# Gate and up products of six of the eight expert quads in one 512-column matmul, with the sigmoid behind both, in an fp32 mixture-of-experts block on one core

## What is computed

```python
def hierarchical_moe(x, w_router_group, w_router_expert, w_gate, w_up, w_down):
    ...
    h = (jax.nn.silu(jnp.einsum('td,edf->tef', xt, w_gate))
         * jnp.einsum('td,edf->tef', xt, w_up)
         * combine[..., None].astype(x.dtype))
    return jnp.einsum('tef,efd->td', h, w_down).reshape(nb_, s_, d_)
```

## Time and profile before

| | us |
|---|---|
| median of three runs | 392.3 |
| the profiled execution, its own time | 392.49 |
| its span in the trace | 390.2 |
| TensorE busy | 358.6 (92%) |
| VectorE busy | 161.3 (41%) |
| ScalarE busy | 138.0 (35%) |
| moved by DMA | 132.79 MB, mean 340 GB/s |

### The profile page before, as it was taken

The page is one execution under the profiler, slowest core; times in us unless marked ns, Lnnn a source line. Parts: engine busy times, 40 slices in busy tenths (PEclk is TensorE's granted clock), DMA queues, the critical chain, the costliest instruction groups (busy, mean ns, idle before and its releaser), DMA issues.

```text
span 390.2 us, 8014 instructions
## 1 busy us (share of the span) xinstructions
PE 358.6 (92%) x3331; PEld 284.4 (73%) x3331; DVE 161.3 (41%) x337; ACT 138.0 (35%) x240; POOL 35.2 (9%) x42
## 2 busy tenths in 40 slices
PE   7999999999999999999899999999599398299995
PEld 7999988999999999998657575656256156157642
DVE  3546579797465656464730303030610111010235
ACT  4643565655535444435723131322112113012012
POOL 3310000000000000001000005207711000000001
PEclk9999999999999999999999999999899699599999
DMA  8699884966759889799899999999999999999962
GB/s 281 204 329 373 302 280 160 349 221 217 269 180 306 279 264 376 228 392 375 306 365 429 425 422 427 425 419 423 426 423 413 427 427 427 427 426 425 412 245 108
DMA packets 52053, 132.79 MB, mean 340 GB/s; under 512 B 2818, under 2 KB 36626, under 8 KB 41012
## 3 DMA queue, kind: packets, MB, share of 16 engines
q1 hardware_dynamic: 51572, 131.88, 87.7%
q0 software_dynamic: 304, 0.17, 0.2%
q10 hardware_dynamic: 144, 0.26, 0.2%
HBM read 131.25 MB, written 1.05 MB: 339 GB/s over the span
## 4 chain that ended last, share of the span: by engine, by line
PE 67%; DMA 16%; SPq 8%; DVE 5%; ACT 2%; issue 1%; DVEq 0%; ACTq 0%
PE bank L1200 15%; DMA gu<-in_w_up 14%; PE bank L1494 10%; PE bank L1229 8%; PE bank L1362 6%; PE bank L1530 6%; PE bank L1232 4%; PE bank L1445 4%; PE bank L1542 4%; SPq L469 4%; SPq L434 3%; PE bank L1344 3%; PE bank L1299 2%; DMA raw<-in_w_in 2%; DVE wl L835 2%
## 5 line engine op out<-in xcount | busy, mean ns | idle before, releaser
L835 DVE TENSOR_TENSOR wl<-raw,wh 128x1024 fp32r<-128x1024 f32 x54 | 65.8, 1223 | 55.0 <-ACT wh L653 54.8
L1494 PE MATMUL bank<-gu,xg 128*32 128x256 f32 x1024 | 61.8, 401 | 20.4 <-DMA gu<-in_w_up 19.8
L653 ACT ACTIVATE wh<-raw 128x1024 fp32r<-128x1024 f32 x54 | 56.5, 1056 | 59.8 <-DMA raw<-in_w_in 20.2
L1494 PEld LDWEIGHTS bank<-gu,xg 128*32 128x32 f32 x1024 | 33.4, 116 | 45.4 <-issue 25.0
L1229 PE MATMUL bank<-xh,wh 128*128 128x256 f32 x176 | 44.1, 288 | 0.5 <-ACT qT L715 0.5
L1229 PE MATMUL bank<-xl,wh 128*128 128x256 f32 x176 | 43.1, 283 | 0.0
L1229 PEld LDWEIGHTS bank<-xh,wh 128*128 128x128 f32 x176 | 33.6, 191 | 2.7 <-issue 2.0
L1097 DVE TENSOR_SCALAR xg<-bank,gcol,bcol 128x128 f32<-128x128 f32 x32 | 10.9, 404 | 59.0 <-PE bank L1445 59.0
L1229 PEld LDWEIGHTS bank<-xl,wh 128*128 128x128 f32 x176 | 33.7, 191 | 0.0
L1445 PEld LDWEIGHTS bank<-pick,x1p 128*128 128x128 f32 x256 | 29.8, 192 | 1.9 <-issue 0.9
L1445 PE MATMUL bank<-pick,x1p 128*128 128x128 f32 x256 | 30.2, 276 | 0.6 <-DVE pick L1068 0.6
(11 more groups left out here) (234 smaller groups left out, 588.7 us busy)
## 6 DMA issues: line engine op xcount, KB each, us to landing
gu<-in_w_up SPq DMA_DIRECT2D x31, 1024.0 KB, 19.6
gu<-in_w_gate SPq DMA_DIRECT2D x30, 1024.0 KB, 15.0
dn<-in_w_down SPq DMA_DIRECT2D x26, 1024.0 KB, 17.6
raw<-in_w_in SPq DMA_DIRECT2D x40, 512.0 KB, 5.6
raw<-in_w_o SPq DMA_DIRECT2D x8, 512.0 KB, 5.0
raw<-in_w_out_conv SPq DMA_DIRECT2D x4, 512.0 KB, 4.0
raw<-in_w_out_attn SPq DMA_DIRECT2D x4, 512.0 KB, 5.0
gu<-in_w_gate SPq DMA_DIRECT2D x1, 2048.0 KB, 10.7
```

Source lines behind the costliest of these rows:

```text
L653: act.activation(wh[:, s, :].rearrange("p (k c) -> p k c", k=KC), raw[pair % NRAW][:, :].rearrange("p (k c) -> p k c", k=KC) [:, :, n % 2 ...
L835: dve.tensor_tensor(wl[:, s, :].rearrange("p (k c) -> p k c", k=KC), raw[pair % NRAW][:, :].rearrange("p (k c) -> p k c", k=KC) [:, :, n % ...
L1494: mm = pe.matmul(bank[6 - part][g, 0:DE], xg[:, k, g], w[:, e, part, k, :], start=(k == 0), stop=(k == KC - 1), skip_group_check=True)
```

## The change

In rounds 1 to 6 each chunk and expert gets one matmul of 512 moving columns, gate and up side by side, where there were two of 256; the result fills all of `bank[6]`, gate in its first half and up in its second. Rounds 0 and 7 keep the separate products, but their up half goes to the second half of `bank[6]` too. `gate_ps` is signalled in round 0 alone (for SyncE's loads of quad 2). The sigmoid waits for `gu_ps`, both products, in every round. VectorE reads the up product from `bank[6]`.

```diff
--- before.py
+++ after.py
@@ -780,7 +780,7 @@
 
             def compute(n):
 
-                act.wait_ge(gate_ps[-1], n)
+                act.wait_ge(gu_ps, n)
                 act.activation(sg[:, :], bank[6][:, 0:DE], ACT.Sigmoid).then_inc(sg_done, 1)
                 act.wait_ge(hT_ps, n)
                 act.activation(hT[:, :, :], bank[4][:, 0:SEQ].rearrange("p (j s) -> p j s", j=FC),
@@ -1124,7 +1124,7 @@
                                   ALU.mult).then_inc(round_link, 1)
                 dve.wait_ge(round_link, 2 * c + 2)
                 dve.wait_ge(gu_ps, c + 1)
-                dve.tensor_tensor(hs[:, :], sg[:, :], bank[5][:, 0:DE],
+                dve.tensor_tensor(hs[:, :], sg[:, :], bank[6][:, DE:2 * DE],
                                   ALU.mult).then_inc(bank_free[6], 1)
                 dve.wait_ge(put_ps, c + 1)
                 pick_slots(coming)
@@ -1473,32 +1473,52 @@
                             pe.wait_ge(gu_in[half], 16 * QE * (2 * loads - (half == 0 and loads > 1)))
                         if q == 2:
                             pe.wait_ge(gate2_in, 16 * len(GATE_PARTS))
-                        for part in range(2):
-                            if last_quad:
+                        def gathered(k):
+
+                            if k < KC // 2:
+                                pe.wait_ge(xg_a, KC // 2 * c + k + 1)
+                            else:
+                                pe.wait_ge(xg_v, KC // 2 * c + k - KC // 2 + 1)
+
+                        def project(k, parts):
+
+                            for e in range(QE):
+                                g = slice(SLOTS * e, SLOTS * (e + 1))
+                                mm = pe.matmul(bank[6][g, parts.start * DE:parts.stop * DE], xg[:, k, g],
+                                               w[:, e, parts, k, :],
+                                               start=(k == 0), stop=(k == KC - 1), skip_group_check=True)
+                            return mm
+
+                        if 0 < q < NQ - 1:
+                            for k in range(KC):
+                                gathered(k)
+                                mm = project(k, slice(0, 2))
+                            mm.then_inc(gu_ps, 1)
+                        elif q == 0:
+                            for i, (lo, hi) in enumerate(GATE_PARTS):
+                                if hi == KC:
+                                    pe.wait_ge(rank_read, 1)
+                                    gather(c, [NK - 1])
+                                for k in range(lo, hi):
+                                    gathered(k)
+                                    mm = project(k, slice(0, 1))
+                                mm.then_inc(gate_ps[i], 1)
+                            for k in range(KC):
+                                mm = project(k, slice(1, 2))
+                            mm.then_inc(gu_ps, 1)
+                        else:
+                            for part in range(2):
                                 for e in range(QE):
                                     pe.wait_ge(last_gu_in[part][e], 16)
                                     if part and e < QE - 1:
                                         stay_warm(WARM_LAST[e])
-                            for k in range(KC):
-                                if last_quad and part == 1 and k == KHALF:
-                                    pe.wait_ge(last_up_end, 16)
-                                if q == 0 and part == 0 and k == KHALF:
-                                    pe.wait_ge(rank_read, 1)
-                                    gather(c, [NK - 1])
-                                if part == 0 and k < KC // 2:
-                                    pe.wait_ge(xg_a, KC // 2 * c + k + 1)
-                                elif part == 0:
-                                    pe.wait_ge(xg_v, KC // 2 * c + k - KC // 2 + 1)
-                                for e in range(QE):
-                                    g = slice(SLOTS * e, SLOTS * (e + 1))
-                                    mm = pe.matmul(bank[6 - part][g, 0:DE], xg[:, k, g],
-                                                   w[:, e, part, k, :],
-                                                   start=(k == 0), stop=(k == KC - 1), skip_group_check=True)
-                                for i, (_, hi) in enumerate(GATE_PARTS):
-                                    if part == 0 and k == hi - 1:
-                                        mm.then_inc(gate_ps[i], 1)
-                            if part == 1:
-                                mm.then_inc(gu_ps, 1)
+                                for k in range(KC):
+                                    if part and k == KHALF:
+                                        pe.wait_ge(last_up_end, 16)
+                                    if not part:
+                                        gathered(k)
+                                    mm = project(k, slice(part, part + 1))
+                            mm.then_inc(gu_ps, 1)
                         pe.wait_ge(pickw_done, 2 * c + 2)
                         for t in range(TT):
                             mm = pe.transpose(bank[7][:, SEQ + t * P:SEQ + (t + 1) * P],
```

## The result

The changed kernel is slower by 0.46% (ratio 1.0046, 95% interval 1.0034 to 1.0058): median 394.16 us of 20 runs against 392.4 us of 20 runs of the kernel before, +1.8 us (+1.3 to +2.3). The forecast was 393.5, +1.24. The profiled execution took 393.78 us, span 391.5.

What follows compares the result with a forecast made beforehand. Expert-weight loads run without a gap to about 378 us; from 365.8 us compute sets the end. Round 6 +0.52, round 7 +0.87, late weights -0.15 make +1.24 us: from 392.3 to 393.5 us, range 392.4 to 394.9.

Steps and rivals of the forecast that it cites:

- The sigmoid behind both products adds 0.87 us a round, and the wide product takes back 0.07: Every round: sigmoid and first multiplication lie between product and `hs`, +0.87 us; 512-column products save 0.07 in rounds 1 to 6.
- The 2.6 us less a round: Wide product: estimate from the Trainium skill's matmul spacing, 4.5 us instead of 7.11; the sum went by the rows instead.
- The table load stays free: ScalarE's table load in the loop (1.28 us) still runs ahead of the sigmoid's wait and adds nothing.
- the rival of the dry queue: SyncE's issue at 247.06: queue empties if rounds 0 to 2 grow over 4.3 us; +4.5 us, 396.8, chance 0.05.
- Round 7, +0.87 less what late weights give back (+0.72): Last round: late sigmoid and multiplication on the path, +0.87 us; less waiting for the last down weights, -0.15.
- Round 6, +0.52: Round 6 lasts 0.80 us longer, TensorE has 0.28 to spare, so the last up product starts 0.52 us later.
- The first rival: Only round 7 counts: TensorE has more to spare at the last up weights, round 6's term vanishes; 393.0 us, chance 0.27.
- Rounds 0 to 5, "Cost 0": Longer rounds are absorbed by idle time before round 4; the later load issue still finds 1.9 us of loads queued; 0 us.
- a digit below 9: Sign against the forecast: DMA's busy digit dropping below 9 in a slice from the 21st to the 38th.

Runs made afterwards that it cites:

- e2: The kernel before with the sigmoid waiting for the end of the up product in rounds 0, 1 and 2 alone: +1.5 us against the kernel before.
- e1: The changed kernel with the 512-column products of rounds 1 to 6 split again into two of 256, sigmoid still behind both: +2.6 us against the kernel before.
- e4: The kernel before with the sigmoid waiting for the end of the up product in round 7 alone: +0.9 us against the kernel before.
- e3: The kernel before with the sigmoid waiting for the end of the up product in rounds 3 to 6 alone: +0.2 us against the kernel before.
- e7: The changed kernel without the six filling matmuls behind the third up load of round 7: +0.8 us against the kernel before.
- e8: The kernel before without the six filling matmuls behind the third up load of round 7: -0.3 us against the kernel before.
- e6: The kernel before with one of quad 4's gate loads (1 MB) issued earlier, ahead of quad 3's down weights: -0.4 us against the kernel before.

## Why the prediction was right and wrong

**Right in the range and the sign** (393.5 forecast, 394.16 measured, in 392.4 to 394.9), and half right in the reason. That the range holds is partly luck. The prediction left out the largest term; had the 1.5 us of e2 come on top of its 1.24 in full, the time would have been 395.0, just outside the range.

- *The sigmoid behind both products adds 0.87 us a round, and the wide product takes back 0.07*: the round's period went from 19.63 us (the sigmoids at 218.62 and 238.25 before) to 20.39, +0.76; expected +0.80. The mechanism is right, and each size is a little off: the late sigmoid adds 0.80 (e1's period of 20.43 against 19.63), because the sigmoid follows the product by 0.03 us and not by the 0.10 that was taken to cancel, and the saving was 0.04. The 2.6 us less a round that the prediction set beside its sum are not in these fp32 rows.
- *The table load stays free*: right, 213.97, ahead of the wait. The drain that the rival of the dry queue mentions does not show: before, the load at 198.45 ends at 199.73, and the sigmoid starts at 199.75.
- *Round 7, +0.87 less what late weights give back (+0.72)*: right for the execution that it was read from, +0.71 there (0.80 less 0.09), and e4 has +0.9. The same term is 0.06 to 0.80 from trace to trace, as the down weights land; the prediction took one value. It also read only the wait at the last down weights (0.40); there is another of 0.54 us at the piece before.
- *Round 6, +0.52*: the mechanism is right, the filling matmuls close up. The up product starts 0.57 us later in the profile, but 0.27 of that is round 6's own later start (339.34 after 339.07), so round 6 gave 0.30, with a product that was 0.16 shorter. Its worth in the timed runs is uncertain, +0.2 in e3 and 0.7 by e7 and e8. The first rival's doubt, that the 0.28 us of slack is one execution's, is borne out by e4 and e6 (none, and 0.64).
- *Rounds 0 to 5, "Cost 0"*: **this is the step that failed.** The working said that the issue at 247.06 had 4.3 us to spare, because `dn_r` landed at 251.4, and that with 2.47 us more "1.9 us of loads" would still be queued. The delay was right: counted from round 0's table load, the issue comes at 50.93 us instead of 48.61, 2.32 us later. The margin was wrong. A landing tells when a load's last part is done, not when the stream of data thins out, and an issue is not yet data: the hole opened over three microseconds before that landing and closed some two microseconds behind the issue. The rival "the load queue runs dry" had the right place and the right mechanism, but the wrong point from which it decides (4.3 us of delay, so only with the table load), and so it got 0.05 and a price of 4.5 us. What it costs at 2.3 us of delay is 1.4 us of loads, and e2 has +1.5. The sign that the prediction had named for this, a digit below 9, did not come, and the mean share from 200 to 360 us stayed at 1.01 (421 GB/s after 424): both were too coarse to see it.

In place of the forecast's sum, the profiled pair has 1.13 (later loads) + 0.30 (round 6) + 0.71 (round 7) = 2.14 us for the experts' part. The timed runs have 1.5 for the hole and 0.2 to 0.7 for round 6; 0.9 for round 7 stands for a kernel without the hole, and behind the hole less of it is left, down to the 0.06 that e2's trace leaves. Added up in full they make 2.6 to 3.1, more than the 1.8 measured; with 0.06 for round 7 they make 1.8 to 2.3. Against that speaks e1, with 2.6 and no wide product. How the rest divides between the overlap, chance and the wide product (0.04 us a round by the rows, 0.6 to 0.8 by the timed runs, whose intervals overlap) stays open. That the profiled executions differ by 1.29, so near to the 1.24 of the forecast, is a coincidence: the changed kernel's started its experts' part 0.86 us early.

## What to carry to other kernels

Read the margin of a load queue from GB/s in windows of a microsecond, not from the last landing, and least of all from a busy digit of a long slice; then keep one more load queued than the landing asks for. Costs measured one by one do not simply add where a late load stands behind them: each hides in the wait that another one causes. A consumer moved behind two producers instead of one costs its own time wherever the chain behind it is waited for, and besides the end of the kernel that includes every place where this chain releases a buffer whose reload is issued just in time. Where matmuls are already spaced by their columns, as here (7.11 and 7.07 us), halving their number gains next to nothing by the rows.

## What the runs showed that was not expected

A load of 1 MB that lands 2.7 us after the next one was issued did not keep the DMA engines busy: 205 and 188 GB/s in two successive microseconds, against 424, and 1 MB issued earlier closed this completely (434 and 418). And taking away six filling matmuls gained the kernel before little (e8, -0.3 us) and the changed one 1.0 us (e7), although nothing about them was changed: once the chain ahead of them is late, filler is work on the path. The gap between the two gains is not clear of noise, but the rows show the filler closing up. The clock did not need them: without them it is 1.00 in e7's round 7.

```profile
365.00:375.00 10.00, 8.58 (x110) 5.40 (x102) 1.58 (x5) 1.04 (x3) 0.00 (x0) 1.00 1.04 405
375.00:385.00 10.00, 9.17 (x55) 4.45 (x52) 5.87 (x13) 2.19 (x5) 1.16 (x2) 1.00 0.24 85
```
